# The token-half differences of the inner tiles, for the sixth down product, made in the down stage from two loads instead of in the up stage

## What is computed

```python
h, ffn_state = _causal_dwconv(ffn_prev, x1 @ p['w_up'], p['ffn_dw_w'], p['ffn_dw_b'])   # width 3
hg, hv = jnp.split(h, 2, axis=-1)
f = (jax.nn.silu(hg) * hv) @ p['w_down']            # D_FF = 2816, D_MODEL = 1024
y = _layer_norm(DN_ALPHA * x1 + f, p['ln2_g'], p['ln2_b'])
```

## Time and profile before

| what | value |
|---|---|
| median of three runs | 2009.12 us (2006.18 to 2009.48) |
| the profiled execution's own time | 2004.44 us |
| its span, first to last instruction | 2002.6 us |
| mean granted clock of TensorE | 0.992 |
| PE / PEld busy | 97% / 89% |
| DVE / ACT / POOL busy | 69% / 42% / 45% |
| up stage, pairs (L3394) | 1326.5 to 1750.6 us |
| down stage (L3475) | 1750.6 to 1994 us |

### The profile page before, as it was taken

How to read it: one execution, slowest core, us unless ns; L and a number is a source line. 1 busy time by engine, 2 the same in 40 slices (tenths; PEclk the granted TensorE clock), 3 DMA queues, 4 the chain that set the end, 5 groups by cost and what they waited for, 6 DMA issues and landing times.

```text
span 2002.6 us, 34425 instructions
## 1 busy us (share of the span) xinstructions
PE 1938.3 (97%) x13332; PEld 1782.6 (89%) x13332; DVE 1377.1 (69%) x1808; ACT 840.1 (42%) x1482; POOL 910.4 (45%) x562
## 2 busy tenths in 40 slices
PE   9999999999998999998999999989999999999998
PEld 8999999999997888886667999889999999977776
DVE  3999999956636647655445323798887777746778
ACT  4222222225335666674334121654544344554441
POOL 4812334421212343124330235678787878645542
PEclk9999999999999999999999999999999999999999
DMA  6422222323541333326573432242232222468655
GB/s 220 152 95 75 86 95 86 100 82 134 163 137 64 128 122 118 101 92 250 216 280 110 152 115 88 85 133 91 81 106 75 86 76 86 134 197 306 198 184 177
DMA packets 203535, 264.08 MB, mean 132 GB/s; under 512 B 22221, under 2 KB 142303, under 8 KB 199277
## 3 DMA queue, kind: packets, MB, share of 16 engines
q1 hardware_dynamic: 185600, 189.38, 29.6%
q0 software_dynamic: 8320, 46.27, 6.0%
q10 hardware_dynamic: 9469, 26.36, 3.5%
HBM read 200.25 MB, written 62.57 MB: 131 GB/s over the span
## 4 chain that ended last, share of the span: by engine, by line
PE 78%; DVE 10%; issue 3%; DMA 3%; ACT 3%; POOL 2%; SPq 1%; ACTq 0%; DVEq 0%; POOLq 0%
PE ps L2739 32%; PE ps L3394 14%; PE ps L3475 6%; PE ps L2932 5%; PE pst L3394 5%; PE pst L3475 2%; PE ps L3146 2%; PE ps L3199 1%; PE pst L3178 1%; DMA tw_d<-wraw 1%; PE pst L3011 1%; POOL tw_raw L1784 1%; DVE hv L2493 1%; PE pst L3181 1%; DVE tfr L2477 1%
## 5 line engine op out<-in xcount | busy, mean ns | idle before, releaser
L1710 POOL TENSOR_TENSOR wlo<-wraw,whi 128x1024 fp32r<-128x1024 f32 x66 | 160.4, 2435 | 388.2 <-ACT whi L981 293.3
L1986 DVE SCALAR_TENSOR_TENSOR pst<-g_ext,wtap,pst 128x512 f32<-128x512 f32 x464 | 306.9, 751 | 0.0
L2739 PE MATMUL ps<-xh,whi 128*128 128x352 f32 x864 | 187.1, 325 | 1.2 <-ACT stat L1075 1.2
L2739 PE MATMUL ps<-xh,wlo 128*128 128x352 f32 x864 | 186.2, 323 | 0.0
L2739 PE MATMUL ps<-xl,whi 128*128 128x352 f32 x864 | 186.0, 323 | 0.0
L2739 PEld LDWEIGHTS ps<-xh,whi 128*128 128x128 f32 x864 | 147.0, 189 | 1.9 <-issue 1.8
L2739 PEld LDWEIGHTS ps<-xh,wlo 128*128 128x128 f32 x864 | 148.3, 188 | 0.0
L2739 PEld LDWEIGHTS ps<-xl,whi 128*128 128x128 f32 x864 | 146.7, 188 | 0.0
L1880 POOL TENSOR_TENSOR wlo<-wraw,whi 128x512 fp32r<-128x512 f32 x60 | 90.8, 1520 | 33.1 <-ACT whi L1501 33.1
L1880 POOL TENSOR_TENSOR wlo<-x1f,whi 128x512 fp32r<-128x512 f32 x60 | 88.4, 1480 | 36.7 <-ACT whi L1501 36.7
L3394 PE MATMUL ps<-resr,whi 128*128 128x264 f32 x480 | 98.0, 286 | 0.0
(11 more groups left out here) (527 smaller groups left out, 5745.7 us busy)
## 6 DMA issues: line engine op xcount, KB each, us to landing
inr<-f_d SPq DMA_DIRECT2D x77, 256.0 KB, 4.1
wraw<-in_w_in SPq DMA_DIRECT2D x37, 512.0 KB, 3.8
f_d<-hv SPq DMA_DIRECT2D x22, 528.0 KB, 2.7
wraw<-in_w_up SPq DMA_DIRECT2D x40, 256.0 KB, 3.7
x1f<-in_w_up SPq DMA_DIRECT2D x40, 256.0 KB, 3.7
wraw<-in_w_down SPq DMA_DIRECT2D x27, 256.0 KB, 4.1
wraw<-tw_d SPq DMA_DIRECT2D x24, 256.0 KB, 3.8
tw_raw<-in_w_down SPq DMA_DIRECT2D x11, 512.0 KB, 3.5
```

What stands on the lines that cost most here:

```text
L1710: nc.gpsimd.tensor_tensor(wlo[:, n % HL, :], wraw[:, n % RAW, :], whi[:, n % HL, :].bitcast(F32), ALU.subtract).then_inc(lo_done, 1)
L1986: half[x] = link(nc.vector.scalar_tensor_tensor(out=dst, in0=src, scalar=tap(k_), in1=pst[:, x, :], op0=ALU.mult, op1=ALU.add))
L2739: last = nc.tensor.matmul(out[:, c, 0:CH], w[:, k, :], x[:, k, c * CH:(c + 1) * CH], start=(k == 0 and x is hi_x and w is wh), stop=(k == ...
```

## The change

The difference is no longer made in `inner(q)` and no longer stored. `s3_d`, `s3_first`, `s3_buf`, `s3_out` and the waits on them are gone, 11 DVE instructions and 11 stores of 256 KB in the up stage among them. In the down stage product 5 is treated as product 2 is: SP loads both token halves of inner tile k, the first into the slot of x, the second into one of the three further slots, and `a_sum(x)` subtracts them in place. That is 11 more loads of 256 KB and 11 DVE instructions in the steps of product 5. The three further slots are now chosen by x mod 3, and the load of one waits until `a_sum(x - 3)` is done. ACT's high part of product 5 now waits for `a_sum(x)` instead of the load.

```diff
-        s3_d = dram("s3_d", [FT // 2, P, S // 2])
...
-        def a_raw2(k):
-            return inr[:, 4 + k % CR, HF:HF + NH]
+        def a_raw2(x):
+            return inr[:, 4 + x % CR, HF:HF + NH]
...
-        P_SUMS, P_COPIED, P_RESIDUAL = (2, 3, 4), {0: 0, 2: 1}, {1: 0, 2: 1, 4: 0, 6: 1}
+        P_SUMS, P_COPIED, P_RESIDUAL = (2, 3, 4, 5), {0: 0, 2: 1}, {1: 0, 2: 1, 4: 0, 6: 1}
...
-            def s3_out(q):
-                sp.wait_ge(l1_v, S3_0 + q + 1)
-                sp.dma_start(s3_d[q], s3_buf(q)).then_inc(xr_out, 16)
...
-                if e == 5:
-                    sp.wait_ge(xr_out, 48 + 16 * (k + 1))
-                    src = s3_d[k]
-                else:
-                    src = rows_of(k + (KH if e in (1, 4, 6) else 0), 1 if e in (2, 6) else 0)
+                src = rows_of(k + (KH if e in (1, 4, 6) else 0), 1 if e in (2, 6) else 0)
                 sp.dma_start(a_raw(x), src).then_inc(f_in[x % FR], 16)
-                if e == 2:
-                    if k >= CR:
-                        sp.wait_ge(l1_v, SUM0 + k - CR + 1)
+                if e in (2, 5):
+                    if x - CR >= 2 * KH:
+                        sp.wait_ge(l1_v, SUM0 + x - 2 * KH - CR + 1)
                     else:
                         sp.wait_ge(w_used, UP_P0 + 7 * (NP - 1) + 6)
-                    sp.dma_start(a_raw2(k), rows_of(k + KH, 1)).then_inc(dn2_in[k % CR], 16)
+                    sp.dma_start(a_raw2(x), rows_of(k + (KH if e == 2 else 0), 1)).then_inc(dn2_in[x % CR], 16)
...
                 if v and q:
                     act.wait_ge(f_out, 16 * q)
-                    act.wait_ge(l1_v, S3_0 + min(q, KH))
...
                 nc.vector.tensor_tensor(hb[1][:, :], hb[0][:, :], hb[1][:, :], ALU.mult).then_inc(f_done, 1)
-                if q < KH:
-                    dve.wait_ge(f_done, q + 2)
-                    dve.wait_ge(xr_out, 48 + 16 * q)
-                    if q == 1:
-                        dve.wait_ge(w_used, up_block(1, 1) + HL + 1)
-                    nc.vector.tensor_tensor(s3_buf(q), hb[1][:, 0:NH], hb[1][:, NH:S], ALU.subtract).then_inc(l1_v, 1)
...
+                if e in (2, 5):
+                    dve.wait_ge(dn2_in[x % CR], DN2_IN0[x % CR] + 16 * raw2_count(x))
                 if e == 2:
-                    dve.wait_ge(dn2_in[k % CR], DN2_IN0[k % CR] + 16 * (k // CR + 1))
-                    ins = nc.vector.tensor_tensor(kept, raw, a_raw2(k), ALU.add)
+                    ins = nc.vector.tensor_tensor(kept, raw, a_raw2(x), ALU.add)
+                elif e == 5:
+                    ins = nc.vector.tensor_tensor(raw, raw, a_raw2(x), ALU.subtract)
...
-                if 2 * KH <= x + 2 < 5 * KH:
+                if 2 * KH <= x + 2 < 6 * KH:
                     a_sum(x + 2)
```

More of the change, by code:

```diff
@@ L307, in program @@
         FR, BR, CR = 8, 8, 3
-        s3_first = at("s3_first", [P, NH], F32, Z + 28160)
-        def s3_buf(q):
-            return inr[:, 0, HF:HF + NH] if q else s3_first[:, :]
         def b_slot(x):
@@ L322, in a_raw, with raw2_count @@
             return inr[:, x % FR, 0:NH]
-        def a_raw2(k):
-            return inr[:, 4 + k % CR, HF:HF + NH]
+        def a_raw2(x):
+            return inr[:, 4 + x % CR, HF:HF + NH]
+        def raw2_count(x):
+            return sum(1 for y in range(x % CR, x + 1, CR) if y // KH in (2, 5))
         s_keep = at("s_keep", [P, KH, NH], F32, X0)
@@ L580, in program @@
         RR_IN0, F_IN0 = 16 * MT, [48, 32, 32, 32] + 4 * [8 * MT]
-        S3_0, SUM0, RS0, RD0 = T_ADD0 + 8, T_ADD0 + 8 + KH, T_HI0 + 8, T_LO0 + 3
+        SUM0, RS0, RD0 = T_ADD0 + 8, T_HI0 + 8, T_LO0 + 3
         RS = {n: RS0 + j + 1 for j, n in enumerate(("11", "22", "samples", "12", "21"))}
@@ L914, in _ @@
             inner_out(0)
-            s3_out(0)
             up_load(1)
@@ L929, in _ @@
                 inner_out(i + 1)
-                if i + 1 < KH:
-                    s3_out(i + 1)
             sample_rows_in(0)
@@ L2525, in with_fifth @@
             def with_fifth(i):
-                if i == 0:
-                    dve.wait_ge(xr_out, 48 + 16)
                 up_add(i, 3, u3, 3, u1)
```

## The result

The changed kernel takes 2014.3 us, the median of 13 runs (2010.5 to 2016.7), against 2006.9 us of the kernel before, run beside it (2002.2 to 2009.5): ratio 1.0036, 95% interval 1.0027 to 1.0044. It is some 7 us **slower**, where the prediction had 0.5 us faster and gave "slower by over 4 us" a chance of 0.07; it lies outside the 2004.3 to 2012.2 us that were to hold eight in ten. The profiled execution took 2014.3 us, with a span of 2012.5 (before: 2004.4 and 2002.6). The profile of before is of one of its faster executions, 2.5 us under its median, and that of the changed kernel is at its median, so the two profiles lie 9.9 us apart where the medians lie 7.4 apart. The three runs behind the 2009.1 us that the prediction started from were slower than most: the thirteen have 2006.9.

What follows compares the result with a forecast made beforehand. PE was taken as the bound, busy 97% of the span; up stage -1.9 us plus down stage +1.4 us gave -0.5 us, 2009.1 to 2008.6 us; own range 2007.3 to 2010, eight in ten within 2004.3 to 2012.2.

Steps and rivals of the forecast that it cites:

- slower by over 4 us: Whole kernel: outcome needing more than the upper bound of rival 2; chance 0.07.
- +1.4 us: Down stage: DVE reaches the tile sums of step 70 late and the end moves equally; bounds 0 to +4.4 us.
- the cover: Product 5: a lead of up to eight steps hides the added loads and subtractions, which cost PE nothing.
- the low part of step 63: Product 5 on DVE: waits for both loads of step 65, so it comes at 1937.2 against 1930.95.
- The load of step 65: Product 5: second load issued 0.4 us after the first, so the subtraction starts at about 1936.5.
- From there on DVE is without slack: From step 70's tile sums to the program's end: PE waits for DVE, so a 1.4 us delay moves the end equally.
- Rival 2: Product 5: DVE's delay at step 63's low part decides, +4.4 us, total +2.5 us, 2011.6 us; chance 0.16.
- -1.9 us: Up stage: removed differences let PE start pair 2 1.9 us earlier; bounds +0.5 to -4.4 us.
- The first difference: Start of the up stage on DVE: without it `tfr` and DVE's backlog come 2.89 us earlier.
- the clock's term: Up stage, pair 1: a 5.0 us PE wait halves the clock and one slow product costs 2.46 us.
- the 2.89 us at pair 1's start: Up stage: `value_right(0)` comes at 1354.26 instead of 1357.15, so PE starts pair 1 2.89 us earlier.
- rival 3: Up stage: POOL and ACT keep their rhythm and the clock takes the rest; total +1.9 us, 2011.0 us; chance 0.14.

Runs made afterwards that it cites:

- up_half: Changed kernel with the second load and subtraction taken out of product 5, up stage as changed; ratio 1.0006 to the kernel before.
- early_norm: Kernel before with row tile 2's normalisation and row tile 3's statistics ahead of DVE's first product 5 tile sum, row tile 3's normalisation two steps earlier; ratio 0.9991.
- late_norm: Changed kernel with the normalisation of row tile 3 moved behind the last two low parts of the down stage; 2010.5 us, ratio 1.0029 to the kernel before.
- loads_only: Changed kernel with both loads per step in product 5 but no subtraction and nobody waiting for the second load; ratio 0.9998 to the kernel before.
- work_only: Changed kernel with product 5's eleven subtractions made from one load and a tile kept in SBUF, no second load; ratio 1.0035 to the kernel before.
- fill_gap: Changed kernel with the first pair's seventh up-stage product computed twice, in the gap before pair 1; ratio 1.0033 to the kernel before.
- up_half_fill: up_half with the first pair's seventh up-stage product computed twice, in the gap before pair 1; ratio 0.9989 to the kernel before.
- The halves: up_half (1.0006), and the kernel before with the changed down stage while the up stage still makes and stores its differences (1.0050).

## Why the prediction was wrong

**The step that failed** is the one behind "+1.4 us": "So I cost loads and subtractions at nothing for PE in product 5; the cover is the lead of up to eight steps", and with it the low part of step 63 at 1937.2. The cover was not counted in the currency that is used up, DVE's own idle time. The added group, in the changed kernel between 1912 and 1967:

```profile
L2530 DVE TENSOR_TENSOR inr<-inr 128x512 f32<-128x512 f32 x11 | 12.0, 1093 | 3.4 <-DMA inr<-f_d 3.4
...
L2666 DVE SCALAR_TENSOR_TENSOR acc_d<-acc_d,sd,b 128x512 f32<-128x512 f32 x2 | 3.2, 1592 | 0.1
```

12.0 us of work came in. From 160 us after the down stage's first matmul to the tile sum, DVE was busy for 37.9 us of 47.6 before and for 52.8 of 56.4 in the changed kernel. So its idle time fell by 6.1 us, from 9.7 to 3.6, and of the 3.6 nearly all are waits for loads ahead of 1926.26; its work grew by 14.9, the 12.0 and 2.9 more in other instructions, such as L2666, 1.59 us against 0.75 of the same shape before. 12.0 + 2.9 - 6.1 = 8.8, and the sum comes 216.4 - 207.6 = 8.8 us later. Some 1.5 of these are probably PE's standing still before product 5: against up_half, which has that too, it is 7.2. The load of step 65, my only cause of delay, decided nothing: DVE was late at step 63 already, at 1942.43 and not 1937.2. The block behind it took 24.2 us, where I had 22.4.

**"From there on DVE is without slack [...], so the end moves by the same"** was right, and is what turned the delay into time. From the tile sum to the end of the span it is 44.5 us before and 45.9 after, and 44.4 to 46.0 in all kernels with the sum in this place; early_norm shows it from the other side, late_norm that PE's wait is not the main cause.

**Why I didn't see it.** Product 2, my nearest row, has the same three loads per step and the same order. But DVE has 19 us of idle time in 50 there (31.12 busy), and no statistics behind. That PE stays busy there said, in one profile, that loads are harmless for PE; loads_only confirms it for product 5, and product 2 itself had a wait of PE in the changed kernel, 1.75 us. It says nothing of what DVE has left at product 5. Rival 2 had the right place and direction ("DVE has only 4.8 us of idle in 27 there" stood in it), but priced the load and two slow instructions, not eleven.

**The up stage's -1.9 us** was not there. The first difference gave its 2.87 us at `tfr` as predicted. Then DVE's four `tfr` instructions took 11.52 us and not 10.34, and the next two small taps 2.47 instead of 1.56, and `value_right(0)` was only 0.7 us earlier against the up stage's start. PE's wait in front of pair 1 was 4.21 us (predicted 5.0) and the clock fell there, as predicted:

```profile
1323.70 11.52 DVE L2463 TENSOR_TENSOR tfr<-tf,resr 128x1056 fp32r<-128x1056 f32 x4
...
1355.01 0.71 DVE L2497 TENSOR_TENSOR uev<-ps,inr 128x528 f32<-128x528 f32 x1
...
1376.61 0.71 DVE L2497 TENSOR_TENSOR uev<-ps,inr 128x528 f32<-128x528 f32 x1
```

`value_right(1)` was done 1.5 us earlier than before, counted from the up stage's start, where I had 2.9; but PE doesn't wait for it any more. Pair 1 itself is the bound, 0.7 us early at its start and 2.8 us slower by the clock (its first two products took 8.75 us, 5.99 before). So the clock's term was about right, 2.46 forecast and 2.76 measured; the term that failed in this stage is the 2.89 us at pair 1's start, which was 0.7. The missing 2.2 us are in DVE instructions that were longer than in their rows, 1.2 in `tfr` and 0.9 in the small taps. Together with the fall that makes rival 3's up stage, nothing gained, though ACT's and POOL's rhythm is not what took it. How much hangs on one such instruction shows in work_only: the next `tfr` took 1.24 us and not 2.38, pair 1 began 1.1 us earlier, after a wait of 3.05 us, and the up stage took 445.4 us although the clock fell there too.

What the fall costs is shown by fill_gap and up_half_fill: without it the up stage is 445.0 and 445.1 us, 2.3 to 2.4 less than before and 2.7 less than in the changed kernel. The rule of the Trainium skill, "TensorE: Matmul & The Clock Gate", "Why this matters for your kernels", which warns of longer idle gaps between bursts, was right for the gap in front of pair 1, at 4.21 us with a fall and at 1.28 without. It doesn't tell which of the shorter ones bring a fall, as the last section shows.

**The halves don't add up exactly.** 1.0006 and 1.0050 make 1.0056 where the changed kernel has 1.0036 (1.0027 to 1.0044). The three intervals allow it, at their ends. That is left open.

## What to carry to other kernels

Before work is added to an engine with a long lead, count its idle time from there to the next point at which it is the bound; that, and not its lead over the consumer, is the cover. And where an instruction has two durations in the trace, as here 0.68 and 1.78 us beside a busy POOL, it is priced by a mean of both (1.09 here), and some more is added for its neighbours. Work that is moved off the critical engine at the start of a stage can be paid back by the clock, if it makes one gap of PE long; filling that gap with repeated matmuls kept the clock up and the up stage 2.3 us shorter here, though not every kernel's time showed it. And a wait of PE near the end needn't be the loss: move the work behind the wait, and see whether the time moves with it.

## What I had not expected

- **The same wait goes with different clocks.** In the changed kernel the clock fell 1 us after a wait of 2.06 us had ended; before, it held after 2.23. In early_norm, whose up stage is that of the kernel before, the first wait of 4.24 us is followed by two matmuls at full speed (0.51 us for both) and slow ones from 0.6 us on, and the next wait, of 3.28, by two that took 0.81 at once. The length of one gap alone doesn't tell whether it falls, and the first matmuls behind it don't either.
- **The cost of a subtraction on POOL.** It took 1.69 us in the mean over eleven, more than DVE's 1.09, and it slowed the chain behind it more than DVE's backlog did. The rule of the Trainium skill, "SBUF — State Buffer", "Who interferes with whom", that a DVE instruction with two SBUF inputs and a GpSimd one that reads SBUF lock each other out, agrees with DVE's 0.68 or 1.78 us for one low part in neighbouring steps. It may also be why moving such a subtraction to POOL relieves DVE less than it seems: DVE's low parts took 1.02 to 1.07 us each there. No run takes this apart.
- **Loads were cheap in product 5.** The DMA share between 1908 and 1945 was 0.82 at 285 GB/s in loads_only, and its time is that of the kernel before.
